# Second layer of a two-layer decoder step: projection, convolution, norms and spatial gating put into one stage

## The reference

```python
def cd_mixer(h, conv_hist, chunk_rows, w_in, conv_w, conv_b, ln_c_g, ln_c_b, ln_v_g, ln_v_b, w_sp, b_sp, w_out):
    proj = h @ w_in                                   # 1024 -> 2048
    a, g, u, v = jnp.split(proj, [D_C, 2 * D_C, 2 * D_C + D_D], axis=-1)      # 512 each
    hist = jnp.concatenate([conv_hist, a * jax.nn.sigmoid(g)], axis=1)
    yc = causal_dwconv(hist, conv_w) + conv_b         # 31 taps for every channel
    yc = jax.nn.silu(layernorm(yc, ln_c_g, ln_c_b))
    new_conv = hist[:, -(CONV_C - 1):]
    v = layernorm(v, ln_v_g, ln_v_b)
    yd = chunk_spatial(u, v, w_sp, b_sp, chunk_rows)  # u * (tril(w_sp) @ v + b_sp), 8 groups, chunks of 128
    y = jnp.concatenate([yc, yd], axis=-1) @ w_out
    return y, new_conv, v
```

## Time and profile before

| | us |
|---|---|
| median of 3 runs (lowest, highest) | 3470.6 (3465.29, 3470.83) |
| the profiled execution's own time | 3478.04 |
| its span, first to last instruction | 3476.3 |
| second layer's projection and convolution, first load to the barrier | 2158.01 to about 2409 |
| norms, spatial gating and split | about 2409 to 2490.12 |
| first load of the output projection | 2490.12 |

### The profile page before, as it was taken

The page is one execution under the profiler, slowest core; times in us unless marked ns, Lnnn a source line. Parts: engine busy times, 40 slices in busy tenths (PEclk is TensorE's granted clock), DMA queues, the critical chain, the costliest instruction groups (busy, mean ns, idle before and its releaser), DMA issues. The chain is left out here.

```text
span 3476.3 us, 60272 instructions
## 1 busy us (share of the span) xinstructions
PE 3113.9 (90%) x24141; PEld 2814.1 (81%) x24141; DVE 1527.1 (44%) x2841; ACT 997.1 (29%) x1901; POOL 976.0 (28%) x643
## 2 busy tenths in 40 slices
PE   4999899899998779999999993993388999999997
PEld 3888576566665779999999982992388999999997
DVE  2341245343444254333333455798455333334335
ACT  3511146344444342111111144111344111111113
POOL 1511157333331442211221123220543212111212
PEclk9999999899999889999999996996699999999999
DMA  6555200255553322111111112110122111111113
GB/s 221 178 188 190 75 1 1 98 166 174 170 166 102 98 91 62 42 48 36 48 42 44 47 52 70 42 35 15 52 79 86 56 36 49 48 42 42 38 36 97
DMA packets 237930, 275.01 MB, mean 79 GB/s; under 512 B 12626, under 2 KB 185547, under 8 KB 237508
## 3 DMA queue, kind: packets, MB, share of 16 engines
q1 hardware_dynamic: 209404, 183.42, 17.0%
q0 software_dynamic: 20992, 75.51, 6.7%
q10 hardware_dynamic: 7376, 13.89, 1.2%
HBM read 248.89 MB, written 24.26 MB: 79 GB/s over the span
## 5 line engine op out<-in xcount | busy, mean ns | idle before, releaser
L498 PE MATMUL ps<-HS,w_split 128*128 128x272 f32 x9600 | 1237.5, 291 | 63.4 <-POOL w_split L856 63.4
L498 PEld LDWEIGHTS ps<-HS,w_split 128*128 128x128 f32 x9600 | 1228.2, 191 | 67.1 <-POOL w_split L856 50.7
L856 POOL TENSOR_TENSOR w_split<-w_raw,w_split 128x1024 fp32r<-128x1024 f32 x144 | 344.5, 2400 | 1228.7 <-ACT w_split L606 1228.6
L506 PE MATMUL ps<-hid,w_split 128*128 128x272 f32 x4224 | 553.0, 291 | 2.9 <-DVE hid L1039 2.9
L506 PEld LDWEIGHTS ps<-hid,w_split 128*128 128x128 f32 x4224 | 539.4, 189 | 7.8 <-DVE hid L1039 3.4
L1108 DVE TENSOR_TENSOR Y<-Y,ps 128x272 f32<-128x272 f32 x576 | 252.2, 438 | 176.0 <-PE ps L506 176.0
L606 ACT ACTIVATE w_split<-w_raw 128x1024 fp32r<-128x1024 f32 x144 | 148.8, 1050 | 505.5 <-PE ps L506 447.6
L1030 DVE TENSOR_TENSOR sg<-sg,ps 128x272 f32<-128x272 f32 x176 | 76.3, 437 | 391.4 <-ACT sg L691 391.4
L1583 PEld LDWEIGHTS ps<-HS_in,w_split 128*128 128x128 f32 x1728 | 223.1, 191 | 31.1 <-issue 17.2
L1583 PE MATMUL ps<-HS_in,w_split 128*128 128x272 f32 x1728 | 234.0, 294 | 11.7 <-POOL HS_in L1744 11.6
L245 PE MATMUL ps<-HS,w_split 128*128 128x272 f32 x1536 | 193.9, 289 | 23.0 <-POOL w_split L222 23.0
(11 more groups left out here) (339 smaller groups left out, 3483.6 us busy)
## 6 DMA issues: line engine op xcount, KB each, us to landing
w_mod_half<-w_mod_in SPq DMA_DIRECT2D x40, 1024.0 KB
w_raw<-w_ffn_gate_in SPq DMA_DIRECT2D x44, 512.0 KB
w_raw<-w_ffn_up_in SPq DMA_DIRECT2D x44, 512.0 KB
w_raw<-w_ffn_down_in SPq DMA_DIRECT2D x44, 512.0 KB
x_part<-x_spill SPq DMA_DIRECT2D x64, 272.0 KB
x_spill<-Y SPq DMA_DIRECT2D x12, 1088.0 KB, 5.5
w_raw<-w_in_ab_in SPq DMA_DIRECT2D x16, 512.0 KB
w_raw<-w_in_cd_in SPq DMA_DIRECT2D x16, 512.0 KB
```

What stands on the lines that cost most here:

```text
L498: ins = pe.matmul(bank(b), wt[:, a, k, :], HS[:, e, k, qs(q)], start=(k == 0 and j == 0), stop=(k == KD - 1 and j == 2))
L506: ins = pe.matmul(bank(b), slots[1 + f][:, a, d * P:(d + 1) * P], hid[:, e, f, qs(q)], start=(f == 0 and j == 0), stop=(f == 1 and j == 2))
L856: pool.tensor_tensor(slots[slot][:, 1, :], raw[u][:, :], slots[slot][:, 0, :].bitcast(F32), ALU.subtract).then_inc(w_lo, 1)
```

## The change

`stage_cd_in` and both blocks of `stage_cd_norms` become one stage `stage_cd`. Its work on PE is a list of 66 units (`CD_UNITS`), each with one PSUM bank of a ring of five (`NBK`):

| units | count | what a unit is |
|---|---|---|
| n = 0 to 7 | 8 | g and a of tile 0, by turns, for each quarter: 24 matmuls of 272 columns |
| 8 to 31 | 24 | g then a of tiles 1 to 3, each four quarters |
| 32 to 40 (NV) | 9 | v token-major: 24 matmuls with 128 tokens as weights and 512 moving columns, which are the four v tiles of the ring |
| 41 to 49 (NS) | 9 | spatial product of one chunk, 8 small matmuls |
| 50 to 65 (NU) | 16 | u, one quarter of all four tiles after another |

Every other engine walks the same numbers n and does at each what is listed for it, so the place in the text is the place in the order. The taps are shared out: of the 31 taps of a tile VectorE takes 25, 22, 20 and 19 (`TAPS_V`), each as two instructions of up to 512 columns, whose running sum is two PSUM banks; for the other 6, 9, 11 and 12 (`TAPS_P`, 38 in all) ScalarE makes the product over about 1000 columns and GpSimd adds it in SBUF. The sample columns are one product over windows (128 x 1984, GpSimd) and one reduction per tile (VectorE) instead of 31 small taps. v needs no transposes, since PE makes it token-major; its gain and bias are folded into the spatial result by VectorE. The mean, variance, scale and sigmoid of y are done per quarter during the u units. Weight buffers (`ring`) are shared with the tail, and the first two tiles of the output projection are loaded and split before the stage ends; `stage_tail` skips them (`ready` = 2). Two rows of parameters more are loaded and transposed at the kernel's start.

```diff
-R_QN, R_KVN, R_CA, R_CB, R_LG, R_LB = 64, 67, 69, 81, 85, 89
-NPARB = 93
+R_QN, R_KVN, R_CA, R_CB, R_LG, R_LB, R_VG, R_VB = 64, 67, 69, 81, 85, 89, 93, 97
+NPARB = 101
...
-def stage_tail(c, HS, l, w_out, spill, nxt, out):
+def stage_tail(c, HS, l, w_out, spill, nxt, out, ring=None):
...
+        ready = 0 if ring is None else 2
...
-            for t in range(KD + 2):
+            for t in range(ready, KD + 2):
                 load(t, src(t), 0, t % 2, t >= 2)
...
-def stage_cd_in(c, HS, yc, U, V):
...
-def stage_cd_norms(c, yc, U, V, HS):
...
+TAPS_P = (6, 9, 11, 12)
+TAPS_V = tuple(CONVC - n for n in TAPS_P)
+def stage_cd(c, HS, ring, w_next):
...
+    hi_after = {t: last_use(t - 4) for t in range(4, len(CD_TILES) + 2)}
+    hi_slot = {t: hi_after[t] if t < 12 else NS for t in range(4, len(CD_TILES))}
+    def steps_by(n):
+        if n < 17:
+            return max(0, min(steps_of[1], 4 * (n - 3)))
+        if n < NV:
+            return min(steps_of[2], steps_of[1] + 4 * (n - 16)) + max(0, 3 * (n - 27))
+        if n < NU:
+            return steps_of[2] + 12 + 58 * (min(n, NS - 1) - NV + 1) // (NS - NV)
+        return min(steps_of[4], steps_of[2] + 70 + 3 * (n - NU + 1))
+    def products_by(n):
+        if n < 16:
+            return max(0, min(6, n - 7))
+        if n < 25:
+            return n - 9
+        if n < NV:
+            return 15 + (n - 24) // 2
+        return min(len(products), 18 + (20 * (n - NV + 1) + 8) // 9)
...
+        MEAN = {NU + 4 + 2 * q: q for q in range(4)}
+        VAR = {NU + 7 + 2 * q: q for q in range(4)}
...
+            def tokens(n):
+                for k in range(KD):
+                    for i, (a, e) in enumerate(((0, 0), (1, 0), (0, 1))):
+                        ins = pe.matmul(bank(n)[0:r].rearrange("p (s n) -> p s n", s=KA), HS[:, e, k, t * P:t * P + r],
+                                        wall[:, 0:KA, a, k * P:(k + 1) * P], start=(k == 0 and i == 0),
+                                        stop=(k == KD - 1 and i == 2))
...
+            def product(m):                                            # ScalarE
+                act.activation(dst[:, d:NPR], z[j][:, 0:NPR - d], ACT.Copy, scale=tap(j, d)).then_inc(prod_made, 1)
...
+            def add(m):                                                # GpSimd
+                acc = pacc[j % 2][:, d:NPR]
+                pool.tensor_tensor(acc, acc, prod[a % 2][:, d:NPR], ALU.add).then_inc(pool_added, 1)
...
+            def step(m):                                               # VectorE
+                if j == 0:
+                    if d >= 1:
+                        dve.wait_ge(conv_step, m)
+                else:
+                    if d > 0:
+                        dve.wait_ge(conv_step, m - 1)
+                acc = c.ps[:, 6 + h, o0:HALF]
+                    ins = dve.scalar_tensor_tensor(out=acc, in0=src, scalar=tap(j, d), in1=acc, op0=ALU.mult, op1=ALU.add)
...
+            def invert(i):
+                dve.reciprocal(rstd[0:r, t:t + 1], rstd[0:r, t:t + 1]).then_inc(v_inv, 1)
+                dve.scalar_tensor_tensor(out=nmr[0:r, t:t + 1], in0=nmr[0:r, t:t + 1], scalar=-1.0, in1=rstd[0:r, t:t + 1],
+                                         op0=ALU.mult, op1=ALU.mult).then_inc(v_inv, 1)
...
+            square(0)                                                  # ScalarE, after the units below NU
+            ln_sqrt(0)
+            high_d(0)
+            square(1)
+            ln_sqrt(1)
+            square(2)
+            silu(0)
+            square(3)
+            silu(1)
+            ln_sqrt(2)
+            ln_sqrt(3)
+            high_d(1)
+            high_c(0)
+            high_d(2)
+            silu(2)
+            to_hi(len(CD_TILES))
+            high_c(1)
+            to_hi(len(CD_TILES) + 1)
+            silu(3)
+            high_d(3)
+            high_c(2)
+            high_c(3)
...
-            V = tile(nc, sc, "V", [P, KA, T])
-            stage_cd_in(c, HS, yc, U, V)
-            stage_cd_norms(c, yc, U, V, HS)
-        stage_tail(c, HS, 1, c.w_out_cd[0], spill, None, True)
+            ring = ([tile(nc, sc, f"w_raw{u}", [P, KD * P]) for u in range(NRAW)],
+                    tile(nc, sc, "w_ring", [P, 4, 2, KD * P], F32R))
+            stage_cd(c, HS, ring, c.w_out_cd[0])
+            stage_tail(c, HS, 1, c.w_out_cd[0], spill, None, True, ring)
```

779 lines of the change are left out of this document (490 added, 289 removed).

## The result

| | before | after |
|---|---|---|
| median of the runs, us | 3470.7 (3465.3 to 3472.3) | 3428.5 (3423.2 to 3432.7) |
| profiled execution, us | 3478.0 | 3427.2 |
| its span, us | 3476.3 | 3425.4 |

The ratio is 0.988, with a 95% interval of 0.986 to 0.990: 42 us faster, where 76 were forecast. The time lies above the upper end of the range (3418). The kernel before has one run more here than in the table that stands ahead of the prediction.

A forecast was written before the change was run, and what follows sets the result against it. VectorE was taken to bound the new stage: last tap at 203.5 us, stage 263.3 instead of 332.1. Gains 68.8 + 7.6 - 0.4 = 76 us gave 3395 us, range 3362 to 3418.

The forecast's parts named there:

- Taps, VectorE's work: New stage up to the last tap: 172 taps on VectorE take 118.5 us, 0.66 or 0.76 us each.
- PE as the bound: Rival for the new stage: taps cost 0.61 us, VectorE keeps up with PE, kernel 3367 us; chance 0.25.
- half rate in PSUM: Rival for the taps: in place in PSUM they take 1.2 us each, kernel 3483 us; slow side's chance 0.04.
- GpSimd near 172: In the v units: GpSimd's window product and 19 additions end near 172 us after the projection's first load, ahead of VectorE.
- Tile 14 is there at about 183: u weight tiles: tile 14 there at about 183 us, tile 15 at 186, PE reaching them at 198 and 201 without waiting.
- Blocking by GpSimd: Mainly in the v units: VectorE's small two-SBUF-input instructions wait for GpSimd's to end, costing 12.5 us.
- The first tap: Start of the new stage: VectorE's first tap comes 25.5 us after the projection's first load.
- The wait for v's last weight tile: End of the a units: PE waits 3.8 us for the tile's split, hidden by VectorE's lag.
- The tail: Last tap to stage end: 59 us, with ScalarE as the chain after the second root and 1 us for gaps.
- The output projection: Its first eight tiles: paced by load and split, 33.2 us, PE needing 25 to 27; gain 7.6 us.
- GpSimd is the bound: Rival for the new stage: GpSimd's additions stretch from 2.35 to 3.55 us, kernel 3410 us; chance 0.2.
- The marks that the prediction gave for itself being wrong: VectorE idle before the last tap, GpSimd additions over 3 us, or last tap and stage end not about 59 us apart.

## Why the prediction was wrong

The stage was 31.1 us longer than forecast: 3.5 before the first tap, 12.9 from the first to the last, 14.6 behind it. The step that failed is the same in all three. The prediction added up one engine's work and took it to run without waits, VectorE's up to the last tap and ScalarE's behind it. The runs showed waits of 11.6 us for the store on VectorE, 13 us for VectorE's results on ScalarE, and 9.0 us for a weight tile ahead of the first gate.

- **Taps, VectorE's work.** Right: 175.5 us busy from the first to the last tap against 178. The length of a tap was guessed from the in-place additions in the earlier trace rows, a form that no row showed, and was right to 10 ns. By start distance the independent taps took 0.65 us (0.66 forecast) and the dependent ones of tile 0 0.82 (0.76); all 172 together took about 120 (118.5). The rivals with other tap costs (PE as the bound, half rate in PSUM) fall with it.
- **The store.** The largest single wait. The sum for VectorE was a sum of busy times and of blocking; it had no term for what its first spatial instruction waits for. The prediction said of this place only that PE may wait for ScalarE or VectorE. The semaphore on the store stands in the code (`v_stored`), and the store stands behind all weight loads in SP's order: 11.6 us. Moving it took the wait away.
- **GpSimd near 172.** It was at 191. It began the v units' part 1.4 us late, the window product and the 19 additions took 3.1 more than forecast, and it waited 14.6 us for ScalarE's products, which for the most part waited for L3021 in turn. That put the loads of tiles 14 and 15, and the store behind them, at 197 to 200. "Tile 14 is there at about 183" was off by 18 us: it was there at 201 and split at 205. The sentence that it causes no wait was true of PE alone.
- **Blocking by GpSimd.** Right as a mechanism, and near in size. Above the 0.16 us of a free one the nine products cost 10.7 us, the four bias additions (L3004) 2.5 above their shortest, and the samples' pair was not blocked: 13.2 where 12.5 were forecast. (Fifteen instructions at 1.1 us in 5 of 6 cases are 13.8; the prediction's own sum is off by 1.3.) Its path through ScalarE was not seen.
- **The first tap.** 3.5 us late. The 25.5 took the first gate as emptied when PE had it. ScalarE's own order, with a weight tile that waits 9.0 us ahead of it, was not walked through.
- **The wait for v's last weight tile.** 6.8 us on PE (L2685) and not 3.8. VectorE was busy beside it, so it was hidden, as said.
- **The tail.** 14.6 us longer. About 2.6 of it come ahead of the second root, 13 as gaps in ScalarE's chain, for which 1 was counted. Work on ScalarE was added up line by line; VectorE's order beside it was not, though it is in-order and interleaved with takes that wait for PE. With that order changed, 9.2 us came back. PE's granted clock after a wait was a term at nothing here: the prediction had the lower clock only in the first microseconds of a stage. Where it did not drop, the tail was 4 us shorter with the order as it was.
- **The output projection.** 5.2 of 7.6. PE needed 29.1 us for the eight tiles and not 25 to 27, at a granted clock of 0.87 over the stretch, and still waited 3.9 for remainders.

The marks that the prediction gave for itself being wrong were the ones that showed: idle time on VectorE before the last tap, and a last tap and a stage end that are not 59 us apart. Its rival "GpSimd is the bound" (3410) was nearest in size, but not by its mechanism, since the additions did not stretch.

## What to carry to other kernels

When several in-order queues are threaded by hand, sum each engine's work, then walk every wait whose releaser is a DMA queue: what stands ahead of that transfer on its queue, and what does that wait for? At each step where an engine both takes a result just being made and does work already ready, the ready work goes first. And when a wait is removed, look at once for what had been done in its shadow; here 4.3 us were given back in the tail, and 3.4 of them returned with GpSimd's order. When a piece in which nothing was edited gets shorter, read the granted clock there before crediting the edit: here that was 4 us in two of the runs.
